# Layer 0's experts in blocks of 32 rows, with rows kept in small on-chip rings

## The reference

```python
def moe_ffn(h, router_w, router_b, w_gate, w_up, w_down):
    probs = jax.nn.softmax((h @ router_w).astype(jnp.float32), axis=-1)
    ...                               # best group of 4 experts, top 2 in it, weights w_sel
    out = jnp.zeros_like(h)
    for e in range(N_EXPERTS):        # 16
        y_e = (jax.nn.silu(h @ w_gate[e]) * (h @ w_up[e])) @ w_down[e]
        out = out + combine[:, e:e + 1] * y_e
    return out                        # w_gate, w_up: 1024 x 512, w_down: 512 x 1024
```

## Time and profile before

| | |
|---|---|
| runs | 1827.09, 1823.35, 1819.29 us; median 1823.35 |
| profiled execution | 1818.96 us, its span 1817.2 us |
| mean granted TensorE clock | 0.964 |
| PE, PEld busy | 1676.3 us (92%), 1016.8 us (56%) |
| DVE, ACT, POOL busy | 712.0, 412.7, 293.1 us |
| moved by DMA | 384.16 MB, mean 211 GB/s |

### The profile page before, as it was taken

One profiled execution on the slowest core, in us unless ns is written; L12 is line 12 of the kernel. 1 busy time (PEld: TensorE's weight loads), 2 busy tenths in 40 slices (PEclk: granted clock), 3 DMA queues, 4 the chain that ended last, 5 costly groups with the idle time before them and its releaser, 6 DMA issues.

```text
span 1817.2 us, 29220 instructions
## 1 busy us (share of the span) xinstructions
PE 1676.3 (92%) x11492; PEld 1016.8 (56%) x11492; DVE 712.0 (39%) x1586; ACT 412.7 (23%) x866; POOL 293.1 (16%) x263
## 2 busy tenths in 40 slices
PE   5999998989999999899999989999789999899975
PEld 2467555554444444465555556676557888455543
DVE  3578864741110112511111158688764111523222
ACT  4011213550000001322222250111044000333321
POOL 0004333860000000300000020044355000000000
PEclk9999988999999999999999988998789999999998
DMA  9410569229221153499999833115671436599995
GB/s 391 141 47 25 173 258 294 63 97 338 92 98 69 70 231 116 181 337 394 381 391 381 313 119 116 47 48 199 213 168 48 162 139 255 234 389 395 410 411 224
DMA packets 107341, 384.16 MB, mean 211 GB/s; under 512 B 40992, under 2 KB 60704, under 8 KB 68064
## 3 DMA queue, kind: packets, MB, share of 16 engines
q1 hardware_dynamic: 85360, 335.44, 49.4%
q0 software_dynamic: 4272, 30.67, 4.9%
q10 hardware_dynamic: 17600, 16.49, 3.1%
HBM read 363.18 MB, written 31.98 MB: 217 GB/s over the span
## 4 chain that ended last, share of the span: by engine, by line
PE 70%; DMA 8%; DVE 7%; POOL 4%; SPq 4%; issue 3%; ACT 3%; ACTq 0%; POOLq 0%; DVEq 0%
PE tile_ps L639 59%; PE out_ps L639 5%; PE turn_ps L639 4%; DMA arena<-sorted_in 4%; SPq L556 3%; POOL arena L2055 3%; DMA vn<-in_wpack 1%; PE turn_ps L964 1%; DVE arena L1919 1%; DMA x<-in_xT 1%; DMA arena<-in_rpb 1%; ACT arena L1399 1%; PE tile_ps L858 0%; DVE smx L1901 0%; SPq L561 0%
## 5 line engine op out<-in xcount | busy, mean ns | idle before, releaser
L639 PE MATMUL tile_ps<-h,ring 128*128 128x512 f32 (+1 forms) x1312 | 477.1, 519 | 5.0 <-ACT h L1177 5.0
L639 PEld LDWEIGHTS tile_ps<-h,ring 128*128 128x128 f32 x1312 | 254.2, 195 | 211.5 <-issue 195.6
L639 PE MATMUL tile_ps<-arena,ring 128*128 128x512 f32 (+1 forms) x704 | 235.3, 486 | 2.7 <-issue 2.7
L639 PE MATMUL tile_ps<-arena 128*32 128x256 f32 (+3 forms) x2096 | 205.3, 387 | 12.1 <-ACT arena L1399 3.8
L639 PEld LDWEIGHTS tile_ps<-arena,ring 128*128 128x128 f32 x704 | 133.6, 190 | 96.6 <-issue 87.6
L639 PEld LDWEIGHTS tile_ps<-arena 128*32 128x32 f32 (+2 forms) x2096 | 122.6, 128 | 56.7 <-issue 29.2
L2055 POOL TENSOR_SCALAR arena<-arena,smx 128x512 f32<-128x512 f32 (+1 forms) x96 | 128.9, 1360 | 65.7 <-DVE smx L1907 65.4
L1372 ACT ACTIVATE arena<-tile_ps 128x512 f32<-128x512 f32 (+1 forms) x56 | 27.4, 490 | 347.3 <-PE tile_ps L639 347.3
L1940 DVE TENSOR_TENSOR arena<-tile_ps,arena 128x512 f32<-128x512 f32 (+1 forms) x32 | 17.9, 558 | 212.1 <-PE tile_ps L639 212.1
L639 PE MATMUL out_ps<-arena 64*128 64x64 f32 (+1 forms) x968 | 82.7, 327 | 7.7 <-issue 7.7
L639 PE MATMUL tile_ps<-h,arena 128*32 128x256 f32 (+1 forms) x336 | 80.6, 483 | 4.8 <-ACT arena L1399 4.8
(11 more groups left out here) (330 smaller groups left out, 2297.9 us busy)
## 6 DMA issues: line engine op xcount, KB each, us to landing
ring<-in_wpack SPq DMA_DIRECT2D x176, 1024.0 KB, 8.5
arena<-in_wpack SPq DMA_DIRECT2D x64, 1024.0 KB, 15.7
h<-in_wpack SPq DMA_DIRECT2D x15, 1024.0 KB, 17.9
qa<-in_wpack SPq DMA_DIRECT2D x12, 1024.0 KB, 15.8
qn<-in_wpack SPq DMA_DIRECT2D x12, 1024.0 KB, 17.7
kn<-in_wpack SPq DMA_DIRECT2D x12, 1024.0 KB, 19.6
vn<-in_wpack SPq DMA_DIRECT2D x12, 1024.0 KB, 22.6
sorted_out<-arena ACTq DMA_DIRECT2D x44, 128.0 KB, 7.9
```

The source lines that it names most:

```text
L639: return nc.tensor.matmul(out, lhsT, rhs, start=start, stop=stop)
```

## The change

Layer 0 also gets blocks of 32 rows, and the row buffers change.

- `gate_up` runs four products side by side: up columns 0 to 127, up 128 to 255, gate 0 to 127, gate 128 to 255, each for 32 rows with 128 moving columns. There are still 8 steps for each of two halves.
- Order on TensorE: both `gate_up` halves, `turn_hidden(0)`, `turn_rows`, `turn_hidden(1)`, then `down` for both halves without anything between them. A down half has 2 steps of four products of 256 moving columns.
- Rows of the next block lie in `hrow` as 128 x 256 (four quarters of the width on four groups of 32 partitions), so two full 128 x 128 transposes turn them.
- `row_ring` and `y_ring` are rings of four blocks on partitions 0 to 31 and 32 to 63 of one arena piece. DVE copies a block from `row_ring` to `hrow` in four pieces; ACT and DVE copy two quarters each of the result to `y_ring`. The ring's place is addressed by a register (`r % 4`).
- POOL loads two blocks with one DMA and stores two blocks with one DMA, from a loop over pairs. ACT issues no result DMAs any more.
- Blocks 0 to 3 are picked by TensorE (four picks of 32 rows in place of two of 64), 2 and 3 of them through `row_ring`.
- `gu_full` counts one per half, `down_full` one per block; SP's waits follow.

```diff
-ROWS_OF = [BS, BS1]
-MAXBLK = 32
-GU_STEPS, DOWN_STEPS = [4, 1], [2, 1]
+MAXBLK = 48
+SORTED = 1792
+RINGED = 4
+GU_STEPS = [2, 1]
...
-        hrow, a7 = cut(a7, [D], parts=BS)
+        hrow, a7 = cut(a7, [256])
...
+        in_and_out, a7 = cut(a7, [RINGED, D])
+        row_ring, y_ring = in_and_out[0:BS1], in_and_out[BS1:2 * BS1]
...
-                    sp.wait_ge(hrow_ready[l], 2)
+                    sp.wait_ge(first_full, RINGED)
...                                                        # TensorE
+                def turn_hidden(r, half):
+                    if half:
+                        pe.wait_ge(ring_in, RINGED)
+                        pe.wait_ge(hid_too, r + 1)
+                    nc.tensor.transpose(hid_bank[half], hid[:, half], c("ident")[0:2 * BS1, 0:2 * BS1])\
+                        .then_inc(turned_hid[l], 1)
...
+                def gate_up(e, r, half, ks):
+                    wg, wu = (arrived(e, half * 2 + n) for n in range(2))
+                    for k in ks:
+                        for q, w in enumerate((wu, wu, wg, wg)):
+                            if (half, k, q) == (1, KD - 1, 3):
+                                pe.wait_ge(hid_done[l], r + 1)
+                            ins = mm(gu_bank[half][group(q)], hsT[:, k % 2, group(k // 2)],
+                                     w[:, k, q % 2 * P:(q % 2 + 1) * P], k == 0, k == KD - 1)
...
-                        gate_up(e, r, 0)
-                        gate_up(e, r, 1)
-                        turn_hidden(0)
-                        turn_rows(range(4))
-                        pe.wait_ge(y_taken[l], r + 1)
-                        down(e, r, 0)
-                        turn_hidden(1)
-                        turn_rows(range(4, KD)).then_inc(turned_in[l], 1)
-                        down(e, r, 1)
+                        gate_up(e, r, 0, range(KD)).then_inc(gu_full[l], 1)
+                        gate_up(e, r, 1, range(KD)).then_inc(gu_full[l], 1)
+                        turn_hidden(r, 0)
+                        turn_rows(r + 1)
+                        turn_hidden(r, 1)
+                        pe.wait_ge(y_taken[l], r + 1)
+                        pe.wait_ge(y_other, r + 1)
+                        down(e, r, 0)
+                        down(e, r, 1).then_inc(down_full[l], 1)
...                                                        # ScalarE
-                    nc.scalar.copy(ysb, y_bank).then_inc(y_taken[l], 1)
-                    act.wait_ge(y_taken[l], r + 2)
+                    act.wait_ge(ring_out, r + 1)
+                    act.wait_ge(down_full[l], r + 1)
                     for n in range(2):
-                        act.dma_start(sorted_out[bass.ds(r * BS, BS)][:, n * 512:(n + 1) * 512],
-                                      ysb[n * BS:(n + 1) * BS]).then_inc(rows_out[l], 16)
+                        ins = nc.scalar.copy(y_ring[:, bass.ds(r % RINGED, 1), n * 256:(n + 1) * 256].rearrange("p a n -> p (a n)"),
+                                             y_bank[n * BS1:(n + 1) * BS1])
+                    ins.then_inc(y_taken[l], 1)
...                                                        # VectorE
+                    dve.wait_ge(ring_in, r + 3)
+                    for q in range(4):
+                        ins = CP(hrow[q * BS1:(q + 1) * BS1],
+                                 row_ring[:, bass.ds(r % RINGED, 1), q * 256:(q + 1) * 256].rearrange("p a n -> p (a n)"))
+                    ins.then_inc(hrow_ready[l], 1)
+                    dve.wait_ge(ring_out, r + 1)
+                    dve.wait_ge(down_full[l], r + 1)
+                    for n in range(2, 4):
+                        ins = CP(y_ring[:, bass.ds(r % RINGED, 1), n * 256:(n + 1) * 256].rearrange("p a n -> p (a n)"),
+                                 y_bank[n * BS1:(n + 1) * BS1])
+                    ins.then_inc(y_other, 1)
...                                                        # GpSimd
+                def load_and_store(pair, first=False):
+                    pool.wait_ge(hrow_ready[l], pair * 2 - 2)
+                    pool.dma_start(row_ring[:, bass.ds((pair + 1) % 2 * 2, 2), :], two_blocks(sorted_in, pair))\
+                        .then_inc(hrow_in[l], 16)
+                    for copied in (y_taken[l], y_other):
+                        pool.wait_ge(copied, pair * 2 - 1)
+                    if not first:
+                        pool.wait_ge(rows_out[l], pair * 16 - 32)
+                    signal(0).then_inc(ring_out, 2)
+                    store(pair - 2, pair % 2)
+                    pool.wait_ge(hrow_in[l], pair * 16 - 16)
+                    signal(3).then_inc(ring_in, 2)
```

More of the change, by code:

```diff
@@ L1056, in _, with pick_rows, turn_rows @@
                     break
[L1058 to L1069, removed]
+                group = lambda q: slice(q * BS1, (q + 1) * BS1)
+                def pick_rows(r):
+                    pe.wait_ge(hot_done, r // 2 + 1)
+                    marks = (hot, hot_next)[r // 2][:, :, r % 2 * BS1:(r % 2 + 1) * BS1]
+                    for n in range(len(tiles)):
+                        for q in range(4):
+                            ins = mm(first_bank[r][group(q)], marks[:, n, :], ht[:, n, q * 256:(q + 1) * 256],
+                                     n == 0, n == len(tiles) - 1)
+                    ins.then_inc(first_full, 1)
+                def turn_rows(r):
+                    pe.wait_ge(hrow_ready[l], r + 1)
+                    for h2 in range(2):
+                        ins = nc.tensor.transpose(rows_bank[:, h2 * P:(h2 + 1) * P], hrow[:, h2 * P:(h2 + 1) * P],
+                                                  c("ident"))
+                    ins.then_inc(turned_in[l], 1)
+                def turn_hidden(r, half):
[4 more added lines that the diff above has]
+                        .then_inc(turned_hid[l], 1)
                 def arrived(e, n):
@@ L1074, in arrived @@
                     return slot if len(slot.shape) == 3 else slot.rearrange("p (k n) -> p k n", k=KD if n < 4 else 2)
-                def gate_up(e, r, half):
+                def gate_up(e, r, half, ks):
                     wg, wu = (arrived(e, half * 2 + n) for n in range(2))
[L1078 to L1088, removed]
+                    for k in ks:
[4 more added lines that the diff above has]
+                                     w[:, k, q % 2 * P:(q % 2 + 1) * P], k == 0, k == KD - 1)
+                    return ins
                 def down(e, r, half):
@@ L2095, in _ @@
+                load_and_store(2, True)
+                with pool.Fori(3, n_pairs + 1) as pair:
+                    load_and_store(pair)
+                for copied in (y_taken[l], y_other):
+                    pool.wait_ge(copied, n_blocks + 1)
+                store(n_pairs - 1, (n_pairs + 1) % 2)
+                pool.wait_ge(rows_out[l], n_pairs * 16)
+                signal(4)
                 for t in tiles:
```

122 lines of the change are left out of this document (58 added, 64 removed).

## The result

| | before | after |
|---|---|---|
| median of 20 runs each | 1827.32 us (1816.68 to 1843.92) | 1816.03 us (1805.44 to 1829.03) |
| ratio | 1 | 0.9928, 95% interval 0.9900 to 0.9957 |
| profiled execution, its span | 1818.96, 1817.2 us | 1823.22, 1821.2 us |
| mean granted clock | 0.964 | 0.956 |

The medians differ by 11.3 us, and the ratio makes it 13. The forecast was 23.4. So the direction was right and the gain is about half of what was forecast; the interval excludes the forecast ratio of 1800 / 1823.35 = 0.987. A few executions are slow throughout, in e7 three of eight and its profiled one among them, and the ratios here leave those out.

What follows compares the result with a forecast made beforehand. TensorE's chain was taken to bound layer 0's experts, with the DMA limit 25 us behind. Terms: 1015.3 - 1041.3 + 1.6 + 1 = -23.4 us, so 1823.35 - 23.4 = 1800 us; forecast 1791 to 1812, range 1784 to 1826.

Steps and rivals of the forecast that it cites:

- Blocks: Layer 0's expert loop: 39 blocks for 22, each 6.36 us (3.44 gate_up, 0.1 shape change, 2.82 tail and down).
- rival 2: Gate and up: 128-column rounds don't get shorter, 0.17 us a round, blocks of 8.4 us, time 1873; chance 0.08.
- rival 1: Address registers or longer ACT loop come last: blocks 7.2 to 7.4 us, time 1831; chance 0.11 for its worse half.
- four drains of 0.1: Tile shape changes in a block: by the skill's rule 39 x 0.4 = 16 us, against the 8 us counted.
- DMA limit and expert ends: Layer 0's experts: weights at 345 GB/s make TensorE wait 5 us; experts' ends add 4 us at most.
- turn 14 wait: Late in layer 0's experts: TensorE waits 5 us for turn 14's weights, so down ends at 1015.
- rival 3: Weights hide the gain: 320 GB/s, time 1817, no change; chance 0.17 together with the better half of (1).
- register loads: At each expert's end, before the next gate_up: 0.3 x 16 = 4 us at most.
- Start: Picks before the first gate_up: 750.39 + 6.9 + 0.45 = 757.8, which is 1.1 us earlier than before.
- four smaller ones have the same passes: Picks at the stage's start: two took 7.09 us, and four of 32 rows were counted at 6.9 us.
- End: Down's end to first gather: 5.8 us for 4.2, so +1.6, from copies, POOL's wait and issue, and landing.
- Landing at least 3.6: Landing of the last result store before the first gather: at least 3.6 us, part of the 5.8 us.

Runs made afterwards that it cites:

- e7: Changed kernel without row loads from block 4 on and without stores except the last; 1807.11 us, median of all eight runs (ratio 0.9840).
- e12: Changed kernel whose layer 0 weight loads of turns 3 to 15 bring 64 of each slot's 2048 columns; 1809.36 us, one run.
- e9: Changed kernel without the scatter of tokens into sorted_in, eight small POOL operations in its place; 1799.89 us, one run.
- e10: Changed kernel with the scatter's eight indexed writes replaced by eight plain writes of the same tiles; 1810.42 us, one run.
- e6: Changed kernel with blocks 2 and 3 picked together, 64 rows by 512 columns; 1818.92 us (ratio 0.9960).
- e5: Kernel before with each gate and up product of 256 moving columns split into two of 128; 1829.29 us (ratio 1.0019).
- e4: Changed kernel, SyncE loading layer 1's first six weight slots only after layer 0's last gather has landed; 1815.92 us (ratio 0.9926).
- e8: Kernel before without its row loads from block 2 on, blocks working on rows in hrow; 1803.25 us in two runs (ratio 0.9858).
- e2: Kernel before with half of each weight slot loaded for turns 3 to 15 of layer 0; 1820.02 us (ratio 0.9954).

## Why the prediction was half right

| term (us, against before) | forecast | measured | off |
|---|---|---|---|
| first pick to first gate_up | -1.1 | 13.0 - 8.5 = +4.5 | +5.6 |
| first gate_up to the end of down | 257.5 - 282.4 = -24.9 | 1030.1 - 769.7 - 282.3 = -21.9 | +3.0 |
| end of down to first gather | +1.6 | 9.3 - 4.2 = +5.1 | +3.5 |
| gathers and adds | +1 | 26.2 - 26.0 = +0.2 | -0.8 |
| sum | -23.4 | -12.1 | +11.3 |

**Blocks: right, but for a slip in the rounds.** 39 of them. The second half with its change of shape was forecast at 1.82 and took 1.8 to 1.9, down with the first half 3.44 and took 3.5, the tail 1.1 and took 1.0 to 1.1. The sum is 6.45 for 6.36, and 39 x 0.09 = 3.5 us covers the whole error of this row. Most of it is a slip in the prediction: its own row gives 0.218 us for a round of 256 columns and so 0.109 for one of 128, but it went on with 0.215 and 0.1075. With 0.218 and 0.109, which is what the rounds took, the block comes to 6.43. Half-width rounds do take half the time (rival 2 falls), and the ACT loop and address registers stay hidden (rival 1 falls): an ACT copy takes 0.362 and TensorE never waits for `hid_done` in the run. By the Trainium skill's rule that I weighed ("TensorEngine Tiling (Array Packing)", Key Properties: a change of tiling mode drains TensorE), four drains of 0.1 would have made 6.56 and my two 6.36. With the rounds put right these are 6.63 and 6.43, and the trace, 6.45, agrees with two that cost time, the other two lying inside a wait.

**DMA limit and expert ends: right in size.** Forecast 5 us of waiting for weights and 4 us at experts' ends; measured 8.6 "over", of which turn 14 has 3.4 and the experts' starts 5.2. The turn 14 wait stood where it was forecast, and rival 3 falls with 341 GB/s. The cause of the 4 us was wrong, though: they are not register loads, which cost nothing in e12, but holes that the weights' transfers make, by the packets above late instructions.

**Start: failed, the largest miss.** The step was "four smaller ones have the same passes", which took the picks' time from their passes alone and put what runs beside them at nothing. The passes were right: without the scatter the first gate_up starts 7.4 us after the first pick (e9), the forecast's own figure (750.39 to 757.8). Beside the indexed scatter it is 13.0. There TensorE got the 64 products of picks 2 and 3 and as many weight loads in 8.8 us, 14.5 per us on average, where it had taken 35 per us in the first two picks, and its signals to VectorE came 4 us late. That the indexed scatter does it is shown (e9, e10). That it does so by the number of instructions is only part of it: e6 has a quarter of the products in these picks and gets back 3.0 of the 5.6 us between first pick and first gate_up, but only 1.0 at the second Silu; and e5 ran 33 per us for 3.9 us beside the same scatter without a hole, with as many products and loads in the scatter's 12 us (228) as the changed kernel. What else the changed kernel's picks have that the kernel before hasn't is their form, 32-column tiles for 64-column ones; no run separates the two, and the mechanism stays open.

**End: mis-sized.** "Landing at least 3.6" was a lower bound taken as the value; it was 6.85 behind six ring loads that I had placed behind the store, and 2.90 without them (e4). By the Trainium skill's fit for a DMA issued from GpSimd ("DMA: Bandwidth & Descriptors", Anatomy of one DMA: 2.0 us and the bytes over 436e3) an estimate for 256 KB is 2.6 us. The undisturbed landing agrees, 2.90; the ones in the weights' traffic, 6.8 and 8.6 in the median for stores and loads, do not. A fit of lone transfers is a lower end where queues are full.

The measured 1816 is near rival 3's 1817, but not by its mechanism. The row ring took the `hrow` wait away, as it should; e8 prices that wait at 9.6 us, and of the 23.4 us forecast for the whole about 9 were given back at the two ends of the stage (5.6 + 3.5), 3 more in the blocks. That the weights' loss came out at 8.6 us for 9 is partly luck, since the larger part of it has another cause than was forecast.

## What to carry to other kernels

Cutting work into smaller blocks multiplies instructions at the same number of passes. Look at two places in the trace then: what TensorE does beside an indexed DMA, and where a loop's new body begins together with a burst of loads. At each end of a stage look at what lands beside the one transfer that is waited for; delaying loads that nobody needs yet (e4) gave 3.4 us in the stage for one line, though no measurable time. And judge changes of under 1% by the stage that was changed and by many runs, not by two spans.

## What the runs showed of the hardware

- Beside an indexed write of 4.2 MB by POOL, TensorE's picks in 32-column tiles came in bursts (14.5 products and loads per us on average) and its signals up to 4.4 us late, 5.8 in e6; beside a plain write of as many bytes in as many packets, with the DMA engines at 1.01, hardly a hole and no late signal (e10). The kernel before and e5, with 64-column tiles, had no hole beside the indexed write and no signal over 0.2 us late. Which part of the indexed form does it was not tried.
- Instructions come in 16 KB packets, and a hole put down to issue ended 1.23 to 1.55 us after a packet's end, 30 times out of 30. Halving the weights didn't help, making them tiny did.
- A hole of 3.77 us was followed by 4.6 us at a granted clock of 0.50, and waits of 2.5 and 0.85 us by some 9 us at 0.65 to 0.70 (e10); after the hole of 1.58 us in the changed kernel it stayed at 1.00.
- A POOL transfer of 256 KB landed in 2.90 us with nothing beside it, in 6.85 beside six loads of 1 MB. Row loads of the kernel before took 7.6 in the median both beside half of the weights (e2) and beside all of them.
